# Products of a hybrid encoder layer run block by block behind norms and splits, with two projections and four u units moved across stages

## What is computed

```python
xn = rms_norm(x, norm1_g)
q, k, v, p_rw, gate_sb, gate_rw = split(xn @ w_in)        # 8 heads of 128 for q, k, v
o_sb = stick_breaking_attention(q, k, v)                   # sample frames also see 512 cached rows
o_rw = rwkv7(p_rw)                                         # 16 heads of 64, in chunks of 64 frames
mixed = sigmoid(gate_sb) * (o_sb @ w_branch_sb) + sigmoid(gate_rw) * (o_rw @ w_branch_rw)
h = x + mixed @ w_out
xf = rms_norm(h, norm2_g)
idx, gate = top 16 of 128 x 128 product keys of xf @ w_q, for 8 heads
h = h + sum over the chosen experts e of gate * gelu(xf . peer_u[e]) * peer_v[e]
y = rms_norm(h, final_norm_g)
```

## Time and profile before

| what | value |
|---|---|
| median of 3 runs | 5068.87 us (5064.38 to 5071.78) |
| profiled execution | 5072.53 us, span of its instructions 5070.7 us |
| TensorE | busy 4757.4 us, 94% of the span |
| VectorE, GpSimd, ScalarE | 3011.3 us (59%), 2258.6 us (45%), 1412.1 us (28%) |
| transfers | 1077.07 MB, 212 GB/s over the span |

### The profile page before, as it was taken

One profiled execution on the slowest core, in us unless ns is written; L12 is line 12 of the kernel. 1 busy time (PEld: TensorE's weight loads), 2 busy tenths in 40 slices (PEclk: granted clock), 3 DMA queues, 4 the chain that ended last, 5 costly groups with the idle time before them and its releaser, 6 DMA issues. The chain is left out here.

```text
span 5070.7 us, 90897 instructions
## 1 busy us (share of the span) xinstructions
PE 4757.4 (94%) x35388; PEld 4575.4 (90%) x35388; DVE 3011.3 (59%) x4666; ACT 1412.1 (28%) x1816; POOL 2258.6 (45%) x878
## 2 busy tenths in 40 slices
PE   6999989999999989969998989999999999999998
PEld 5999888888888889969998879999999999999997
DVE  4333255555555633345877856647777777777775
ACT  3333322222212221122233323323332333333332
POOL 3222222121211123334443235547877777777873
PEclk8999999999999999989999999999999999999999
DMA  6999733333323366962233365538888878888883
GB/s 233 334 340 338 277 104 128 118 128 119 104 86 108 108 197 209 352 239 91 99 113 143 143 222 188 160 121 301 292 303 290 306 285 305 292 299 298 293 303 126
DMA packets 343249, 1077.07 MB, mean 212 GB/s; under 512 B 99344, under 2 KB 153104, under 8 KB 263952
## 3 DMA queue, kind: packets, MB, share of 16 engines
q1 hardware_dynamic: 291264, 783.02, 44.9%
q0 software_dynamic: 36864, 268.45, 14.2%
q10 hardware_dynamic: 14928, 22.84, 1.2%
HBM read 876.90 MB, written 197.29 MB: 212 GB/s over the span
## 5 line engine op out<-in xcount | busy, mean ns | idle before, releaser
L154 POOL TENSOR_TENSOR wlo<-raw,whi 128x2048 fp32r<-128x2048 f32 x170 | 792.0, 4659 | 2141.7 <-ACT whi L150 2141.7
L168 POOL TENSOR_TENSOR wlo<-raw,whi 128x1024 fp32r<-128x1024 f32 x432 | 1042.1, 2412 | 503.3 <-ACT whi L164 495.4
L164 ACT ACTIVATE whi<-raw 128x1024 fp32r<-128x1024 f32 x432 | 458.1, 1060 | 1041.2 <-PE psS L236 409.4
L236 PE MATMUL accs<-xh,whi 128*128 128x272 f32 x2624 | 581.6, 303 | 69.6 <-DMA at_before<-in_cst 40.6
L2147 DVE SCALAR_TENSOR_TENSOR Y<-R,HD,Y 128x2048 f32<-128x2048 f32 x127 | 460.2, 3624 | 217.5 <-DMA R<-in_v,IDX 212.0
L236 PE MATMUL accs<-xh,wlo 128*128 128x272 f32 x2624 | 548.9, 291 | 0.0
L236 PE MATMUL accs<-xl,whi 128*128 128x272 f32 x2624 | 548.5, 291 | 0.0
L236 PEld LDWEIGHTS accs<-xh,whi 128*128 128x128 f32 x2624 | 420.8, 192 | 93.1 <-issue 58.8
L236 PE MATMUL psS<-hh,wlo 128*128 128x416 f32 x1408 | 497.0, 353 | 0.0
L236 PE MATMUL psS<-hh,whi 128*128 128x416 f32 x1408 | 495.1, 352 | 0.0
L236 PE MATMUL psS<-hl,whi 128*128 128x416 f32 x1408 | 492.9, 350 | 0.0
(11 more groups left out here) (397 smaller groups left out, 9746.4 us busy)
## 6 DMA issues: line engine op xcount, KB each, us to landing
raw<-in_u SPq DMA_DIRECT2D x128, 1024.0 KB, 5.0
raw<-in_v SPq DMA_DIRECT2D x128, 1024.0 KB, 5.8
raw<-in_w_in SPq DMA_DIRECT2D x82, 1024.0 KB, 8.0
at_UI<-in_u SPq DMA_DIRECT2D x64, 1024.0 KB, 8.9
u_d<-at_UO SPq DMA_DIRECT2D x256, 256.0 KB, 6.2
g_d<-STG SPq DMA_DIRECT2D x8, 3328.0 KB, 10.3
Ge<-g_d SPq DMA_DIRECT2D x64, 416.0 KB, 8.4
wo_UI<-in_u SPq DMA_DIRECT2D x24, 1024.0 KB, 9.1
```

The lines of the kernel that those rows point to most:

```text
L154: pool.tensor_tensor(self.lo[:, c % 2, :], self.raw[:, c % 2, :], self.hi[:, c % 2, :].bitcast(F32), ALU.subtract).then_inc(self.split_don ...
L164: act.activation(self.half(self.hi, c, h), self.half(self.raw, c, h), ACT.Copy).then_inc(self.hi_done, 1)
L168: pool.tensor_tensor(self.half(self.lo, c, h), self.half(self.raw, c, h), self.half(self.hi, c, h).bitcast(F32), ALU.subtract).then_inc(se ...
L236: mm = pe.matmul(out, w(k), x(k, n), start=a, stop=z)
```

## The change

- `norm` takes a product `then`. TensorE runs its first unit block by block behind each low part, a second unit straight behind it in "n2". All low parts are VectorE's now. "n1" runs the first head's Q projection, "n2" the first two u units; "n2" also loads w_q's first two units (`following`) and splits the first.
- In attention the loop starts at K (`range(1, 3)`), and the next head's Q projection, `project(UNITS)`, stands between the `tri` products and the product with WT. Behind the last head this is RWKV's first projection, which is gone from there.
- In mix the first unit's product waits for one low part at a time. Behind the last unit TensorE runs the output projection's first unit in the same way behind mix's low parts.
- In the output projection VectorE waits for X in four parts, and adds before it transposes.
- TAIL is 26 instead of 22, so PRE is 44: 2 u units in "n2", 16 in the heads of retrieval, 8 behind them. The expert stage has 42 phases with gathered rows instead of 44, and every fourth may hold seven rows.

TensorE in attention, before: from the last `tri` products to the end of a head (SPL and WT are the scores' logarithms and weights, VTM is V by tokens, CV the cached V).

The diff, cut to its core:

```diff
@@ -263,7 +263,7 @@
-        counts = {"attention": 4 * HEADS, "rwkv": 6 * PAIRS + 2, "mix": KB, "out": KB, "retrieval": 2 * PH + TAIL, "gates": 2 * GB_N}
+        counts = {"attention": 4 * HEADS, "rwkv": 6 * PAIRS + 2, "mix": KB, "out": KB, "n2": 2, "retrieval": 2 * PH + TAIL - 2, "gates": 2 * GB_N}
         base, at = {}, 0
@@ -276,7 +276,7 @@
                 norm(nc, S, "n1", A, par, eps, psS, X, C_N1, src=lambda a, b: A["xT"][:, a:b, :], hi=xh, lo=xl, W=W,
-                     ahead=[A["w_in"][0], A["w_in"][8]])
+                     ahead=[A["w_in"][0], A["w_in"][8]], then=lambda pe: unit_product(pe, W, 0, acc[0], xh, xl))
             rows = attention(nc, S, A, O, W.phase(0), [A["w_in"][48], A["w_in"][49]], acc, psS, psR, xh, xl, gates_d, o_d, u_d)
@@ -285,11 +285,18 @@
             load_h = lambda a, b: h_d[a:b].rearrange("k p t -> p k t")
-            rows = mix(nc, S, A, W.phase(base["mix"]), [A["w_out"][0], A["w_out"][1]], acc, psS, psR, hh, hl, gates_d, o_d, u_d, rows)
+            rows = mix(nc, S, A, W.phase(base["mix"]), [A["w_out"][0], A["w_out"][1]], acc, psS, psR, hh, hl, gates_d, o_d, u_d, rows,
+                       lambda pe: unit_product(pe, W.phase(base["out"]), 0, acc[0], hh, hl))
             with ExitStack() as ctx2:
                 X = ctx2.enter_context(nc.sbuf_tensor("X2", [P, KB, T], F32))
-                out_projection(nc, S, A, W.phase(base["out"]), [A["w_q"][0], A["w_q"][1]], acc, psS, hh, hl, X, u_d, rows)
-                norm(nc, S, "n2", A, par, eps, psS, X, C_N2, hi=hh, lo=hl, keep=load_h)
+                out_projection(nc, S, A, W.phase(base["out"]), [A["u"][0], A["u"][1]], acc, psS, hh, hl, X, u_d, rows)
+                W2 = W.phase(base["n2"])
+
+                def two_units(pe):
+                    for c in range(2):
+                        yield from dense_product(pe, W2, c, acc[c][:, 0, 0:TD], hh, hl)
+                norm(nc, S, "n2", A, par, eps, psS, X, C_N2, hi=hh, lo=hl, keep=load_h, W=W2, then=two_units,
+                     following=[A["w_q"][0], A["w_q"][1]])
             IDX, GT = sbk("IDX", [P, P], U32), sbk("GT", [P, P])
@@ -323,6 +330,8 @@
                     sp.dma_start(keep(4 * q, 4 * q + 4), X[:, 4 * q:4 * q + 4, :]).then_inc(sem("kept"), 16)
+                for c, unit in enumerate(following):
+                    W.load(sp, unit, c + 2)
                 sp.wait_ge(sem("kept"), 64)
@@ -350,11 +359,8 @@
                     act.activation(hi[:, k, :], XT[:, k % 4, :], ACT.Copy).then_inc(sem("hi"), 1)
-
-        def split_lo(eng, k):
-
-            eng.wait_ge(sem("hi"), k + 1)
-            eng.tensor_tensor(lo[:, k, :], XT[:, k % 4, :], hi[:, k, :].bitcast(F32), ALU.subtract).then_inc(sem(f"lo{k % 2}"), 1)
+            if following:
+                W.split_hi(act, 2)
@@ -362,10 +368,8 @@
                     W.split_lo(pool, c)
-            if hi is not None:
-                for k in range(1, KB, 2):
-                    pool.wait_ge(sem("scaled"), k + 2)
-                    split_lo(pool, k)
+            if following:
+                W.split_lo(pool, 2)
@@ -378,6 +382,16 @@
                 mm.then_inc(sem("summed"), 1)
+            if then is not None:
+                steps = then(pe)
+                for k in range(KB):
+                    pe.wait_ge(sem("lo"), k + 1)
+                    mm = next(steps)
+                mm.then_inc(W.used, 2)
+                for mm in steps:
+                    pass
+                if following:
+                    mm.then_inc(W.used, 2)
@@ -393,14 +407,16 @@
                     if k >= 4 and hi is not None:
-                        dve.wait_ge(sem(f"lo{k % 2}"), (k - 4) // 2 + 1)
+                        dve.wait_ge(sem("lo"), k - 3)
                     if k >= 4 and out is not None:
...
                                              ALU.mult, ALU.mult).then_inc(sem("scaled"), 1)
-                if hi is not None and k >= 2 and k % 2 == 0:
+                if hi is not None and k >= 2:
                     dve.wait_ge(sem("scaled"), k)
-                    split_lo(dve, k - 2)
+                    dve.wait_ge(sem("hi"), k - 1)
+                    dve.tensor_tensor(lo[:, k - 2, :], XT[:, (k - 2) % 4, :], hi[:, k - 2, :].bitcast(F32),
+                                      ALU.subtract).then_inc(sem("lo"), 1)
@@ -506,7 +522,7 @@
                     mm.then_inc(W.used, 2)
-                for u in range(3):
+                for u in range(1, 3):
                     project(u)
@@ -547,6 +563,7 @@
                 tri(lambda b: z_at(0, b * P), (0, 1, 2, 3), cols).then_inc(S["tri_ready"], 1)
+                project(UNITS)
@@ -778,7 +795,6 @@
                     pass
-            run(project(0, 0, 0))
             run(project(1, 0, 0))
@@ -1303,18 +1319,31 @@
         def _(pe):
-            with pe.Fori(0, KB // N) as i:
+            def block_pair(i, first=False):
                 for u in range(N):
...
                     for g in range(2):
-                        pe.wait_ge(S["mx_o_lo"], 8 * g + 8)
+                        if first and u == 0:
+                            pe.wait_ge(S["mx_o_lo"], 8 * g + 1)
+                        done = 8 * g
                         for mm in product(pe, [ps[u][g][:, h, 0:H2] for h in range(2)], lambda k: W.hi[:, u, (8 * g + k) * P:(8 * g + k + 1) * P],
...
                                           lambda k, h: ol[:, 8 * g + k, h * H2:(h + 1) * H2], 8):
-                            pass
+                            done += 1
+                            if first and u == 0 and done < 8 * g + 8:
+                                pe.wait_ge(S["mx_o_lo"], done + 1)
                     mm.then_inc(W.used, 2)
+            block_pair(0, True)
+            with pe.Fori(1, KB // N) as i:
+                block_pair(i)
+            pe.wait_ge(S["mx_mixed"], 2 * (KB - 2) + 6)
+            pe.wait_ge(S["mx_lo_part"], 1)
+            for k, mm in enumerate(first_of_out(pe)):
+                if k + 1 < KB:
+                    pe.wait_ge(S["mx_lo_part"], k + 2)
+            mm.then_inc(W.used, 2)
@@ -1402,14 +1431,19 @@
             add_squares(1, True)
-            with pe.Fori(0, KB // N) as i:
+
+            def block_pair(i, first=False):
                 for u in range(N):
-                    pe.wait_ge(S["wo_sum"], N * i + u + 1)
-                    for mm in unit_product(pe, W, u, acc[u], mh, ml, N, i):
-                        pass
-                    mm.then_inc(W.used, 2)
+                    if not first or u:
+                        pe.wait_ge(S["wo_sum"], N * i + u + 1)
+                        for mm in unit_product(pe, W, u, acc[u], mh, ml, N, i):
+                            pass
+                        mm.then_inc(W.used, 2)
                     pe.wait_ge(S["wo_square"], N * i + u + 1)
                     add_squares(1 - u)
+            block_pair(0, True)
+            with pe.Fori(1, KB // N) as i:
+                block_pair(i)
             pe.wait_ge(S["wo_square"], KB + 1)
@@ -1429,14 +1463,15 @@
             R.start(dve)
-            dve.wait_ge(S["wo_x"], 64)
-            with dve.Fori(0, KB // N) as i:
-                for u in range(N):
-                    for c in range(1 + u):
-                        R.turn(dve, u + c, i)
-                    W.wait_used(dve, u, N, i)
-                    h = halves(flat(N * i + u))
-                    dve.tensor_tensor(h, acc[u][:, :, 0:H2], h, ALU.add).then_inc(S["wo_sum"], 1)
+            for q in range(4):
+                dve.wait_ge(S[f"n1loaded{q}"], 32)
+                with dve.Fori(2 * q, 2 * q + 2) as i:
+                    for u in range(N):
+                        W.wait_used(dve, u, N, i)
+                        h = halves(flat(N * i + u))
+                        dve.tensor_tensor(h, acc[u][:, :, 0:H2], h, ALU.add).then_inc(S["wo_sum"], 1)
+                        for c in range(1 + u):
+                            R.turn(dve, u + c, i)
@@ -1507,7 +1547,6 @@
         def _(pe):
-            pe.wait_ge(S["tk_cst"], 48)
             with pe.Fori(0, PH) as i:
@@ -1521,6 +1560,7 @@
                 block(0)
+                pe.wait_ge(S["tk_cst"], 48)
                 for u, ps in enumerate((psS, psR)):
@@ -1548,10 +1588,10 @@
         def _(act):
-            act.sem_inc(S["tk_q"], 2)
+            act.sem_inc(S["tk_scores"], 2)
             for u in range(2):
-                act.sem_inc(S[f"tk_kept{u}"], 16)
-            act.sem_inc(S["tk_scores"], 2)
+                act.activation(GEL[:, u, :], acc[u][:, 0, 0:TD], ACT.Gelu).then_inc(S["tk_q"], 1)
+            W.split_hi(act, 1)
             act.wait_ge(S["tk_set"], 3)
@@ -1682,7 +1722,7 @@
-TAIL = 2 * PH + 6
+TAIL = 2 + 2 * PH + 8
 START = 2
@@ -1831,7 +1871,7 @@
         for j in range(GROUPS - FIRST):
-            in_u, in_v = 4, 2 if j else 0
+            in_u, in_v = 4, 2 + j % 4 // 3 if j else 0
             nv = min(dotted - summed, 3 if dotted < P else in_u + in_v)
@@ -2175,12 +2215,13 @@
                 coef_lo(2 * g + 3)
```

(9 more changed lines are left out.)

24 lines of the change are left out of this document (14 added, 10 removed).

## The result

| what | value |
|---|---|
| before | 5070.32 us, median of 4 (5064.38 to 5072.03) |
| changed | 5143.14 us, median of 4 (5135.80 to 5148.95) |
| ratio | 1.0145, 95% interval 1.0126 to 1.0164 |
| profiled execution of the changed kernel | 5148.64 us, span 5146.8 us |
| forecast | 5108.0, range 5078.0 to 5134.0 |

The change costs 1.45%. Slower was forecast, but 0.8%, and the measured time lies 9 us outside the range. So the direction was right, and the question is where another 35 us went (38 us in the profiled executions that the next tables compare).

What follows compares the result with a forecast made beforehand. TensorE, busy 94%, was taken as the bound, with attention's load chain only 3 us ahead. Terms 48.1 - 2.4 + 4.5 - 14.1 + 3 = +39.1 us on the median 5068.9 gave 5108 us, range 5078 to 5134.

Steps and rivals of the forecast that it cites:

- the load chain: Attention: SyncE's loads queued behind a head's last product make SPL ready 49.0 us after it, setting the changed head's time.
- R: Attention: the moment a head's last product is done, marked by ScalarE's copy of the output; forecast 141.8 us for the first head.
- Attention, 74.5 us a head: Attention: each head takes 74.5 us, 7.6 more than now; with RWKV's -12.0 the sum is +48.1 us.
- I take 2 us per head: Attention: cost of TensorE's slow clock behind its wait for SPL, 2 us per head.
- The output projection, +4.5: Output projection: later start 2.6 us plus slow clock 1.9 after a wait of some 14 us for the third weight, +4.5.
- Cover of 3 us, so nothing: Output projection: transposing after the sum delays stores and the weight behind them, but 3 us of cover remain; cost nothing.
- Rival C: Attention as forecast, output projection's later transposes delay every second weight by 3 us, v rows cost 8: 5134 us; chance 0.09.
- The second norm, +4.3: Second norm into retrieval: the first projection of retrieval ends at 2293.2 us instead of 2288.9, +4.3.
- The count of u units: Expert stage and retrieval: four u units leave the expert stage, -36.8 us; two go behind retrieval's heads, +18.4.
- +3, bounds 0 and 8: Expert stage: six and five v rows in the last two phases cost some 1 us each and delay a scale, +3 us.
- A: Attention: load chain shrinks, SPL ready under 40 us after a head's last product, heads 63.1 us, total 5014 us; chance 0.11.
- B: Attention: load chain shrinks half way, SPL 43.5 us after a head's last product, heads 69 us, some 5070 us; chance 0.06.

## Why the prediction was right and wrong

- **What bounds the kernel, and the load chain.** Right for the changed kernel. VectorE's last SPL step started 45.7 to 49.6 us after R (forecast 48), TensorE's work from R to tri was 40 us, and the wait 6.6 to 9.7 us against 9. Opening the queue before R took it away; filling the wait did not move SPL. The reading of the kernel before was half of it: there ScalarE's chain ended with the load chain, and it is the projection's move that parted the two.
- **Attention, 74.5 us a head.** It was 76.1, and the first R 143.5 instead of 141.8. The step that failed is the term "I take 2 us per head" for the clock. The piece behind the wait took 23.5 us in the mean over seven heads, and 59.63 - 39.91 = 19.7 us where nothing was waited for: 3.8 us a head. One row of a single wait, cut off after 4 of its 5.8 slow microseconds, had been taken for a constant; here it was 1.6 to 8.0. The upper bound of 3 us was too low as well. The upper bound of a head, 76.1 us, held only because it also took the largest offset of SPL.
- **RWKV.** -13.8 for -12.0.
- **The norm.** A block on VectorE alone: 16 blocks start within 2342.5 - 2323.8 us, 1.25 us apart, for 1.37 forecast, and 1.33 apart in the first norm. In the second norm of the kernel before they were 1.42 apart, so the saving is real. The longest scaling there fell from 1852 to 797 ns (the lines for n2XT above), so 1.27 us was not VectorE's own pace. The Q product in the first norm bought nothing, as said: `tri` of the first head started at 116.83 for 116.3, 1.6 us earlier than before and not 2.1.
- **Mix.** -2.3 for -2.4.
- **The output projection, +4.5.** It was +22.5. The wait for the third weight was right (15.2 for 14). The step that failed is "Cover of 3 us, so nothing" for the transposes behind the sum. That cover was gone in every fourth unit (2.4 to 2.9 us and the clock behind). The last pair's transposes and stores pushed the border back by 5.3 us, and I had not looked at that. Together it is 18.4 us by the run that undoes the order. Rival C, with a chance of 0.09, had the late weights. That its 21 us come so near is partly luck: a wait of 3 us at every second weight and no border was its sum, and there were three such waits and the border.
- **The second norm, +4.3.** +1.6. The sign given for it was incomplete: of the wait of 40.6 us before retrieval 19.4 remain, for the first low part, besides the forecast gaps between the blocks (3.1 us in all, under 1 us each) and one of 2.3 us for a Gelu.
- **The count of u units.** The retrieval part was right (+18.3 for +18.4). In the expert stage the step "+3, bounds 0 and 8" failed, and it measured 14.4. I costed the last two phases, which with the stage's end took 2.5 us more. I left out the nine that the rule fills to seven rows, 8.6 us in all, and the 3.1 us in the first two phases. Why the first rows came later there stays open.
- **Rivals.** A said that heads of 63.1 us are possible if SPL comes less than 40 us after R. It did not happen, since the bytes between R and SPL stayed behind R, but the experiment reached it to the tenth, in five heads, by moving them. Its rate of 412 GB/s was not fanciful: 387 and 409 GB/s held over 36 and 37 us. The Trainium skill, DMA: Bandwidth & Descriptors, Where 436 GB/s comes from, gives 435 GB/s as the ports' ceiling; the 409 measured here is under it. B did not happen.
- **The range.** It ended at C with attention at its forecast size. Three terms erred in the same direction. Attention with RWKV (+59.1) stayed under its own bound of +60 and the output projection (+22.5) under C's 25.5, but the range did not let both come true at once: with both, and the 8 of the v rows, it would have ended near 5146.
